# The decay terms of two attention heads in other row groups of TensorE, alternating

## The reference, cut to what matters

```
c = cumsum(log_sigmoid(u @ w_in[:, 3072:3080] + b_forget), over time)    # one row per head, 256 long
logits[h, t, s] = q[h, t] . k[h, s] / 8 + c[h, t] - c[h, s]              # s <= t, else -inf
p = softmax(logits, over s);  o = p @ v
```

## Time and profile before

| | |
|---|---|
| median of 3 runs | 1803.66 us (1802.46 to 1804.40) |
| the profiled execution | 1803.53 us, its span 1801.6 us |
| TensorE busy | 1653.7 us, 92% of the span |
| VectorE, ScalarE, GpSimd busy | 52%, 38%, 12% |
| mean granted TensorE clock | 0.947 |
| read from HBM | 239.54 MB |

### The profile page before, as it was taken

The page is one execution under the profiler, slowest core; times in us unless marked ns, Lnnn a source line. Parts: engine busy times, 40 slices in busy tenths (PEclk is TensorE's granted clock), DMA queues, the critical chain, the costliest instruction groups (busy, mean ns, idle before and its releaser), DMA issues.

```text
span 1801.6 us, 25993 instructions
## 1 busy us (share of the span) xinstructions
PE 1653.7 (92%) x11161; PEld 1427.0 (79%) x11161; DVE 930.9 (52%) x1256; ACT 690.5 (38%) x981; POOL 220.5 (12%) x202
## 2 busy tenths in 40 slices
PE   4899999999999979999689999999997897889997
PEld 3886898899999978875457778878876794689997
DVE  3532454565655556776653533333326777465454
ACT  4424543533433334215652422222223425543433
POOL 2000100020000002992200000000000690000000
PEclk8998999999999989999769899999998998999999
DMA  7466446556455543235203343343333320045552
GB/s 244 123 205 210 148 159 231 167 129 199 143 185 165 186 141 117 86 126 188 24 1 125 114 136 117 117 140 117 117 116 95 117 95 24 25 141 187 182 170 71
DMA packets 228474, 242.27 MB, mean 134 GB/s; under 512 B 13000, under 2 KB 222248, under 8 KB 228232
## 3 DMA queue, kind: packets, MB, share of 16 engines
q1 hardware_dynamic: 226256, 236.99, 39.8%
q0 software_dynamic: 1568, 2.37, 1.6%
q10 hardware_dynamic: 536, 1.25, 0.2%
HBM read 239.54 MB, written 1.05 MB: 134 GB/s over the span
## 4 chain that ended last, share of the span: by engine, by line
PE 82%; DVE 9%; ACT 4%; DMA 3%; issue 1%; POOL 0%; DVEq 0%; ACTq 0%; SPq 0%
PE bank L654 20%; PE bank L656 20%; PE bank L655 20%; PE score_banks L1022 3%; PE bank L1055 2%; DVE w_lo L642 2%; PE score_banks L1568 2%; PE bank L1038 2%; DVE small L1097 1%; PE bank L726 1%; PE score_banks L1569 1%; PE score_banks L1570 1%; PE score_banks L1026 1%; PE score_banks L726 1%; DMA raw<-in_w_exp_down 1%
## 5 line engine op out<-in xcount | busy, mean ns | idle before, releaser
L642 DVE TENSOR_TENSOR w_lo<-raw,w_hi 128x2048 fp32r<-128x2048 f32 (+1 forms) x176 | 407.3, 2321 | 315.7 <-ACT w_hi L631 315.2
L654 PE MATMUL bank<-xn_hi,w_hi 128*128 128x256 f32 (+1 forms) x1280 | 425.2, 332 | 19.8 <-DVE xn_lo L838 8.9
L655 PE MATMUL bank<-xn_lo,w_hi 128*128 128x256 f32 (+1 forms) x1280 | 420.7, 329 | 0.0
L656 PE MATMUL bank<-xn_hi,w_lo 128*128 128x256 f32 (+1 forms) x1280 | 420.6, 329 | 0.0
L631 ACT ACTIVATE w_hi<-raw 128x2048 fp32r<-128x2048 f32 (+1 forms) x176 | 331.9, 1888 | 165.9 <-PE bank L656 99.1
L654 PE MATMUL bank<-hid_hi,w_hi 128*128 128x256 f32 (+1 forms) x928 | 284.1, 306 | 3.9 <-DVE w_lo L642 1.6
L655 PE MATMUL bank<-hid_lo,w_hi 128*128 128x256 f32 (+1 forms) x928 | 282.0, 304 | 0.0
L654 PEld LDWEIGHTS bank<-xn_hi,w_hi 128*128 128x128 f32 x1280 | 245.7, 192 | 45.9 <-issue 11.0
L656 PE MATMUL bank<-hid_hi,w_lo 128*128 128x256 f32 (+1 forms) x928 | 281.9, 304 | 0.0
L656 PEld LDWEIGHTS bank<-xn_hi,w_lo 128*128 128x128 f32 x1280 | 245.5, 192 | 21.2
L655 PEld LDWEIGHTS bank<-xn_lo,w_hi 128*128 128x128 f32 x1280 | 245.8, 192 | 20.3
(11 more groups left out here) (291 smaller groups left out, 2372.8 us busy)
## 6 DMA issues: line engine op xcount, KB each, us to landing
raw<-in_w_ada SPq DMA_DIRECT2D x48, 1024.0 KB, 5.0
raw<-in_w_in SPq DMA_DIRECT2D x30, 1024.0 KB, 5.1
raw<-in_w_gate SPq DMA_DIRECT2D x22, 1024.0 KB, 5.0
raw<-in_w_up SPq DMA_DIRECT2D x22, 1024.0 KB, 5.2
raw<-in_w_exp_gate SPq DMA_DIRECT2D x16, 1024.0 KB, 5.4
raw<-in_w_exp_up SPq DMA_DIRECT2D x16, 1024.0 KB, 5.4
raw<-in_w_exp_down SPq DMA_DIRECT2D x16, 1024.0 KB, 4.8
raw<-in_w_down SPq DMA_DIRECT2D x16, 1024.0 KB, 4.7
```

Source lines behind the costliest of these rows:

```text
L642: dve.tensor_tensor(w_lo[:, r % RAW_SLOTS, 0:k * cols], raw[:, r % RAW_SLOTS, 0:k * cols], w_hi[:, i % HIGH_SLOTS, 0:k * cols].bitcast(F32 ...
L654: pe.matmul(o, s_hi, m_hi, start=i == 0, stop=False)
L655: pe.matmul(o, s_hi, m_lo, start=False, stop=False)
L656: last = pe.matmul(o, s_lo, m_hi, start=False, stop=i == n - 1)
```

## The change

The running sums are kept at two places of the partitions: rows 0 to 7 and again rows 64 to 71. To get them there the forget weights have 72 columns for each chunk (8 of the weights, 56 of zeros, the same 8 once more), and every operation of the log gates runs on 72 rows in place of 8. Each decay product now contracts over the 64 partitions of the half in which the head's own queries lie, and the additions are issued in alternating order: first addition of head h, first of head h + 1, second of h, second of h + 1, then the two masks. GpSimd clears `bf` and `wf` ahead of "constants", loads the bias twice, waits for the forget weights after its last issue and copies them to the second place; `pe_forget` waits for that copy. `condt` moves to another place in the same scratch tile.

```diff
-        wf = work[:, 0:KC * FOX_H].rearrange("p (k c) -> p k c", k=KC)
+        wf = work[:, 0:KC * F_ROWS].rearrange("p (k c) -> p k c", k=KC)
...
                 for x in (h, h + 1):
-                    extra = [(cT[:, 0, t * P:(t + 1) * P], ident[:, x:x + 1].broadcast_to([P, nk]), 0, nk),
-                             (ident[:, x:x + 1].broadcast_to([P, P]), cT[:, 1, 0:nk], 0, nk),
+                    r = head_rows(x)
+                    pick = lambda n: ident[r, r.start + x:r.start + x + 1].broadcast_to([HD, n])
+                    extra = [(cT[r, 0, t * P:(t + 1) * P], pick(nk), 0, nk), (pick(P), cT[r, 1, 0:nk], 0, nk),
                              (ident, const("causal"), nk - P, P)]
...
-                    for s, sc in zip(unit["s"], unit["subs"]):
-                        for left, right, c0, width in sc["extra"]:
+                    for n in range(len(unit["subs"][0]["extra"])):
+                        for s, sc in zip(unit["s"], unit["subs"]):
+                            left, right, c0, width = sc["extra"][n]
...
-        F_PSUM = bank[6][0:FOX_H, 0:S]
-        f_log = rows[0:FOX_H, 0:2, :].rearrange("h a b -> h (a b)")
+        F_PSUM = bank[6][0:F_ROWS, 0:S]
+        f_log = rows[0:F_ROWS, 0:2, :].rearrange("h a b -> h (a b)")
...
-            pe.wait_ge(*setup_loaded.at("wf"))
+            pe.wait_ge(*pool_done.at("wf"))
...
+            pool.memset(bf, 0.0)
+            pool.memset(wf, 0.0)
             pool.memset(cT[:, :, :], 0.0).then_inc(*pool_done.mark("constants"))
             load_vectors(pool, rows2_loaded, VEC_ROWS[:6])
...
+            pool.wait_ge(*pool_done.at("constants"))
+            for r in (0, HD):
+                pool.dma_start(bf[r:r + FOX_H], a["b_forget"].rearrange("a (h o) -> (a h) o", o=1))\
+                    .then_inc(*wf_loaded.mark(("bf", r), 16))
+            pool.dma_start(wf[:, :, 0:FOX_H], a["w_in"][0, :, 3072:3080].rearrange("(k p) c -> p k c", p=P))\
+                .then_inc(*wf_loaded.mark("all", 16))
...
+            pool.wait_ge(*wf_loaded.at("all"))
+            pool.tensor_copy(wf[:, :, HD:F_ROWS], wf[:, :, 0:FOX_H]).then_inc(*pool_done.mark("wf"))
             pool_stick(pool)
```

More of the change, by code:

```diff
@@ L21 @@
 FOX_H = 8
+F_ROWS = 64 + FOX_H
 HD = 64
@@ L259, in mixer_program @@
         small = sb("small", [P, P])
-        condt = work[:, 64:64 + 2 * KC].rearrange("p (k s) -> p k s", k=KC)
+        condt = work[:, 1024:1024 + 2 * KC].rearrange("p (k s) -> p k s", k=KC)
         amp = small[:, 96:96 + 4 * KC].rearrange("p (i s k) -> p i s k", i=2, s=2)
-        wf = work[:, 0:KC * FOX_H].rearrange("p (k c) -> p k c", k=KC)
+        wf = work[:, 0:KC * F_ROWS].rearrange("p (k c) -> p k c", k=KC)
         wr = sb("wr", [P, KC, GROUPS + EXPERTS])
@@ L292, in mixer_program @@
         esink = lambda s, n=1: small[:, 24 + s % 8:24 + s % 8 + n]
-        bf = small[0:FOX_H, 32:33]
+        bf = small[0:F_ROWS, 32:33]
         sink = small[:, 40:48]
@@ L312, in mixer_program @@
         setup_loaded = signal("setup_loaded")
+        wf_loaded = signal("wf_loaded")
         nat_loaded = signal("nat_loaded")
@@ L1701, in dve_forget @@
             dve.wait_ge(*pool_done.at("constants"))
-            c, minus = cT[0:FOX_H, 0, :], cT[0:FOX_H, 1, :]
+            c, minus = cT[0:F_ROWS, 0, :], cT[0:F_ROWS, 1, :]
             own.ready(dve.tensor_scalar(minus, F_PSUM, bf, 0.0, ALU.add, ALU.min))
             own.ready(dve.tensor_tensor(minus, minus, f_log, ALU.subtract))
-            own.ready(dve.tensor_tensor_scan(c, ones_row[0:FOX_H, :], minus, 0.0, ALU.mult, ALU.add))
+            own.ready(dve.tensor_tensor_scan(c, ones_row[0:F_ROWS, :], minus, 0.0, ALU.mult, ALU.add))
             dve.tensor_scalar(minus, c, -1.0, None, ALU.mult).then_inc(*dve_misc.mark("forget"))
@@ L1906, in _ @@
             pool.memset(cond[:, :, :], 0.0)
+            pool.memset(bf, 0.0)
+            pool.memset(wf, 0.0)
             pool.memset(cT[:, :, :], 0.0).then_inc(*pool_done.mark("constants"))
             load_vectors(pool, rows2_loaded, VEC_ROWS[:6])
-            pool.dma_start(bf, a["b_forget"].rearrange("a (h o) -> (a h) o", o=1)).then_inc(*setup_loaded.mark("bf", 16))
-            pool.dma_start(wf[:, :, :], a["w_in"][0, :, 3072:3080].rearrange("(k p) c -> p k c", p=P))\
-                .then_inc(*setup_loaded.mark("wf_", 16))
+            pool.wait_ge(*pool_done.at("constants"))
[4 more added lines that the diff above has]
+                .then_inc(*wf_loaded.mark("all", 16))
             pool.dma_start(sink, a["attn_sink_2"].rearrange("l h -> (l h)").partition_broadcast(P))\
@@ L1923, in _ @@
             pool.dma_start(bias_row[:, GROUPS:], a["b_router_expert"][:, :]).then_inc(*setup_loaded.mark("br2", 16))
-            for name in ("wf", "all"):
-                setup_loaded.counts[name] = setup_loaded.n
+            setup_loaded.counts["all"] = setup_loaded.n
+            pool.wait_ge(*wf_loaded.at("all"))
+            pool.tensor_copy(wf[:, :, HD:F_ROWS], wf[:, :, 0:FOX_H]).then_inc(*pool_done.mark("wf"))
             pool_stick(pool)
```

## The result

| | before | changed kernel |
|---|---|---|
| median, first comparison | 1804.03 us (1802.46 to 1806.14, 4 executions) | 1791.78 us (1789.96 to 1796.93, 4 executions) |
| ratio | | 0.9935, 95% interval 0.9918 to 0.9953 |
| the profiled execution, its span | 1803.53 us, 1801.6 us | 1796.93 us, 1795.2 us |
| mean granted TensorE clock | 0.947 | 0.952 |

The account below looks back on a forecast made before the run. TensorE was taken to bound the Fox stage, almost without a break. From 1803.53 us, -5.2 (decay pairs) and -0.2 (forget logits) gave 1798.1, or 1798.2 us with the shown median 0.1 higher; range 1796.0 to 1801.6 us.

Parts of the forecast that it names:

- The pairs: Fox stage decay products: two heads' 64-row products run together at one head's price, saving 5.2 us.
- Both rivals on TensorE's order: Fox stage decay products: nothing overlaps (1803.5 us, chance 0.06), or strict program order within pairs (about 1799.5 us, 0.07).
- strict order inside a pair: Fox stage: one extra instruction step per run of pairs, 1.3 us less gain, about 1799.5 us; chance 0.07.
- What is late next: Fox stage: other waits of TensorE keep their cover, so all gain comes through; otherwise a cost of 0 to 2.6 us.
- The copy for the modulation sums: Fox stage, ScalarE's L755 needed by L733: 0.9 us of cover left after a t = 0 unit shortens by 0.45 us.
- The transfers: Fox stage: the same bytes in 5.2 us less raise the rate from 236 to 279 GB/s, without delay.
- The rival of another engine taking half of the gain: Fox stage: another engine or a transfer takes half of 5.4 us, about 1800.8 us; chance 0.05.
- The forget logits: Forget product, weights 8 to 72 columns: width costs nothing; leaving and entering the 8-column form saves 0 to 0.3 us, taken 0.2.
- The start: GpSimd's extra memsets, DMA issue, wait and copy at the front: cost 0 to 0.5 us, taken as 0.
- The clock: Half-clock stretch after the Fox stage may lengthen: 1800.7 to 1803.2 us (0.07) or about 1808 us (0.03); chance 0.10 in all.
- main case: Whole kernel: 1798.2 us, itself between 1796.2 and 1799.8 us as low stretches shift elsewhere; chance 0.72.
- the longer low stretches: Behind the Fox stage: low clock half as long again takes 2.5 us of gain, as long again 5 us; chance 0.07.

Follow-up runs that it names:

- a_zero: Changed kernel plus one 128-row product per head and unit that adds zeros to the scores; 1798.67 us, ratio 0.998.
- b_front: Changed kernel with decay products over 128 rows, head by head, as before, so only its new gates, weights and start remain; 1802.99 us, ratio 0.9996.
- a_again: Changed kernel run a second time, no edit, against the kernel before; 1797.56 us, ratio 0.9955.
- fills: Seven products of constants added where TensorE waits between 145 and 180 us; changed kernel 1796.65 us, kernel before 1800.84 us.
- shifts: Zero products added to the Fox stage: 1.3 us in the kernel before, 1805.03 us; 1.7 us in the changed kernel, 1800.07 us.
- a_headwise: Changed kernel with the additions head by head again, 64 rows kept; 1807.39 us, ratio 1.0023.
- a_third: Changed kernel run a third time, no edit, against the kernel before; 1796.08 us, ratio 0.9955.

## Why the prediction was right, and where it was wrong

**The pairs: right.** Forecast 4 x (0.45 + 0.86) = 5.2 us, measured 5.25 in all three profiles of the changed kernel, per unit 0.44 and 0.86. Both rivals on TensorE's order fell: in a_zero four more instructions of 128 rows per unit take exactly what the pairs save (1.53 and 2.38 us again), so a pair costs no more than one of its products, and the step of 0.11 or 0.22 us more per run that a strict order inside a pair would add is absent. The earlier trace rows show more than the prediction read from them. The two heads' products there aren't neighbours in the program: `pe_stick` has head 0's L1160 and L1161, then head 1's L1160 and L1161. Yet all four instructions of L1160 start (from 159.35) before the first of L1161 (159.88). So head 1's L1160 ran beside head 0's, and ahead of head 0's L1161. "TensorE: Matmul & The Clock Gate" in the Trainium skill, Part 2 and Part 3, has matmuls start and end strictly in program order. For 64-row products of the two halves this case's traces disagree: by the starts in the earlier trace rows, and by the pitch after, where four instructions take 0.43 us as two of one head did.

**What is late next: right.** The copy for the modulation sums kept its 0.9 us: in the timeline of the profile after it ends at 139.33 (L758, 138.95 for 0.38 us) and L736 starts at 140.23. The transfers rose to 267 GB/s, not far from the 279 worked out, and the chain has no wait for one in this stage. The rival of another engine taking half of the gain is refuted: the Fox stage is shorter by the whole 5.25 us.

**The forget logits: at the top of their bounds.** The last eight instructions ahead of the forget product before, then the timeline after:

```profile
39.98 1.15 PE L1786 MATMUL score_banks<-cst,proj 128*128 128x128 f32 x8 [0.20 <-ACT xT L1799]
```

```profile
39.61 1.15 PE L1790 MATMUL score_banks<-cst,proj 128*128 128x128 f32 x8 [0.19 <-ACT xT L1803]
40.59 3.62 PE L1692 MATMUL score_banks<-sq,work 128*72 128x256 f32 x16
43.86 0.47 PE L657 MATMUL bank<-xn_hi,w_hi 128*128 128x256 f32 x1
44.16 0.28 PE L658 MATMUL bank<-xn_lo,w_hi 128*128 128x256 f32 x1
```

From the start of the forget product to that of the second product behind it are 3.57 us (40.59 to 44.16), and before 3.77 (41.06 to 44.83): 0.2 us less, all of it on leaving the forget product. Entering it gives another 0.1: from the start of the eight instructions ahead to that of the forget product are 0.98 us (39.61 to 40.59) in place of 1.08 (39.98 to 41.06). So both halves that the prediction thought of are there, 0.3 us in sum, the top of its bounds, where it took 0.2. The sixteen instructions take 3.27 us to the next start in place of 3.55, so the 3.5 us that the prediction named were off.

**The start: nothing lost.** TensorE reached the forget product 0.5 us sooner than before (40.59 and 41.06), but that isn't steady: without the new front the profiles have it between 40.69 and 41.29, with it between 40.26 and 41.73. b_front, which has the whole front, measures as the kernel before (0.9996), so what the front gives is under what can be told.

**The clock: this is the step that failed.** In the sum it stands at nothing. As a rival the prediction counted it at 0.10 and, save for one sentence, as a loss; its other shifts were priced at "a us or two", and that became the main case's own range. Three things were wrong with that. First, the spread of single executions: the three times before lay 1.9 us apart, but 107 executions lie between 1795.35 and 1808.89 us, and the changed kernel's 23 between 1789.96 and 1804.39. A median of four of them has no claim to within 2 us. The forecast, 1798.2, lies in the upper group of the changed kernel's executions, the 1791.78 in the lower one. Second, the size: the stretch of 165.8 to 175.9 us that I had priced as up to 5 us costs 4.4, and most of this can go: in the profile after 2.9 us of it went. Third, the sign: the longer low stretches were given 0.10, and a gain of more than 2 us no chance at all. What the runs showed in its place: the same program takes 3.5 us more or less in the stick-breaking stage, and 3.4 us more or less between 795 and 809 us, as low stretches fall there or don't. a_again, with the short form of both, has a span 10.4 us shorter than that of before: 5.25 in the Fox stage, 2.9 in the stick-breaking stage, 1.1 ahead of both and 1.2 behind. The three executions of the first four that made the median weren't profiled, so that they had the same is likely and not shown.

By code the change saves about 5.5 us (5.25 + 0.3), which puts the changed kernel at 1797.7 us in the mean: inside the range. The mean measured is 1795.7, just under its 1796.0. 7.5 us were measured, 2 us more, known to 1.9, and 6.8 +/- 2.1 without the first four executions. Whether these 2 us are a steady gain from the clock isn't settled. For it: a_zero, with the Fox stage as long as before, still lies 3.7 us below before, and two of three profiles of the changed kernel have the short stick-breaking stage. Against it: the third has the long one, b_front has the short one and gains nothing, and the rest took 2 to 4.5 us more than in the two profiles of before in two of the three of the changed kernel. The fills and shifts moved low stretches but didn't make the totals follow, and more executions, not another kernel, would be needed to tell 2 us from nothing.

## What to carry to other kernels

In this kernel small products of 64 rows paid only when no product over all 128 rows stood between them and a partner in the other half: the row split alone made this kernel's Fox stage 3 us longer, the order alone changed nothing, with both together two of them take the time of one. The earlier trace rows have a pair with another 64-row product between its two in the program, so strict alternation may be more than is needed; decay products head by head, with both masks behind them, weren't run. Group the work by row width, since each step between 64 and 128 rows costs 0.2 us. And where the trace shows stretches at a lower granted clock, take the range of a forecast from the spread of many executions of the kernel and from the full price of these stretches in both directions, before trusting a sum of instructions to the microsecond.

## What the runs showed of the hardware that wasn't expected

- Each change between 64 and 128 rows costs about 0.2 us (0.38 us for the two more per unit of a_headwise), one half ahead of the change and one behind it; in the prediction only one half of the way from 64 to 128 was seen, 0.10 us.
- A 64-row product of one half started ahead of an earlier one of the other half: in the earlier trace rows head 1's L1160 (one of the four that start from 159.35 on) before head 0's L1161 (159.88).
- The same place of the same program, reached at nearly the same time, got the granted clock 0.50 in one execution and 0.94 in another (159.9 to 170.1 us in a_third and a_again); their stick-breaking stages differ by 3.5 us. At 796.5 to 806.7 us it was 0.50 and 1.00 (after and a_again), and 3.4 us were lost by it.
- A low stretch of 10.2 us cost the stick-breaking stage 4.4 us, but two of 3.4 us only 1.5. The second of them (189.0 to 192.4 us in the profile after) reaches beyond the stage's end at 190.7; that the rest is hidden where TensorE waits anyway is only argued, from its 32.42 busy of 37.40 us.
- Sixteen instructions with 8 weight columns between products with 128 cost 0.3 us more than the same with 72 columns (0.1 on entering, 0.2 on leaving), in every one of the 14 profiles that has the one or the other; the sixteen themselves start 0.22 us apart in both.
